# Two transformer blocks on one core: the scaling of the sixteen gate tiles moved from VectorE to GpSimd

## What is computed

```python
u = rms_norm(h, mix_pre_g[i])
proj = u @ w_in[i]
(q_a, c_kv, q_idx, k_idx, w_idx, q_h, f_h, i_h, g_h, gate_a, gate_b) = split_cols(proj)
...
merged = (jax.nn.sigmoid(gate_a + b_gate[i, :D]) * (y_a @ w_br_a[i])
          + jax.nn.sigmoid(gate_b + b_gate[i, D:]) * (y_b @ w_br_b[i]))
h = h + rms_norm(merged @ w_out[i], mix_post_g[i])
```

## Time and profile before

| | us |
|---|---|
| three runs | 2024.76, 2026.54, 2027.18 |
| median | 2026.54 |
| the profiled execution | 2031.31 |
| its span in the trace | 2029.4 |
| PE busy | 1861.8 (92%) |
| DVE busy | 1167.6 (58%) |
| ACT busy | 648.5 (32%) |
| POOL busy | 201.2 (10%) |

### The profile page before, as it was taken

One profiled execution on the slowest core, in us unless ns is written; L12 is line 12 of the kernel. 1 busy time (PEld: TensorE's weight loads), 2 busy tenths in 40 slices (PEclk: granted clock), 3 DMA queues, 4 the chain that ended last, 5 costly groups with the idle time before them and its releaser, 6 DMA issues.

```text
span 2029.4 us, 23515 instructions
## 1 busy us (share of the span) xinstructions
PE 1861.8 (92%) x8254; PEld 1489.2 (73%) x8254; DVE 1167.6 (58%) x1772; ACT 648.5 (32%) x960; POOL 201.2 (10%) x150
## 2 busy tenths in 40 slices
PE   5887989999999999999899998877789999999996
PEld 4665777777888888888677776666567788888874
DVE  6447658888534755532443776576683755452266
ACT  4333412222223222222333334444353322222242
POOL 3121000000000000000033344243000000000000
PEclk9888999999999999999899999977899999999997
DMA  3431222223222222323222331310152222232221
GB/s 136 79 67 42 73 80 89 92 92 101 100 98 83 93 93 97 103 100 100 78 83 73 114 129 59 114 68 32 47 161 83 73 96 101 93 119 100 92 71 54
DMA packets 55340, 180.61 MB, mean 89 GB/s; under 512 B 6216, under 2 KB 6984, under 8 KB 55272
## 3 DMA queue, kind: packets, MB, share of 16 engines
q1 hardware_dynamic: 43200, 157.07, 23.2%
q10 hardware_dynamic: 12072, 22.67, 4.0%
HBM read 167.65 MB, written 12.06 MB: 89 GB/s over the span
## 4 chain that ended last, share of the span: by engine, by line
PE 68%; DVE 19%; issue 6%; ACT 3%; DMA 2%; POOL 1%; DVEq 1%; ACTq 0%; SPq 0%; POOLq 0%
PE bank L721 16%; PE bank L722 16%; PE bank L723 16%; PE bank L743 2%; PE bank L744 2%; PE bank L809 2%; PE bank L745 2%; PE bank L810 2%; PE bank L811 2%; DMA raw<-in_w_proj 1%; DVE sq L1990 1%; PE bank L1078 1%; PE bank L789 1%; DVE w_lo L1711 1%; DVE chunk L1809 1%
## 5 line engine op out<-in xcount | busy, mean ns | idle before, releaser
L1142 ACT ACTIVATE w_hi<-raw 128x1024 fp32r<-128x1024 f32 (+2 forms) x281 | 304.4, 1087 | 742.7 <-PE bank L723 677.8
L721 PE MATMUL bank<-a_hi,w_hi 128*128 128x512 f32 x1272 | 504.1, 396 | 17.9 <-DVE w_lo L1711 7.7
L723 PE MATMUL bank<-a_hi,w_lo 128*128 128x512 f32 x1272 | 496.8, 391 | 0.0
L722 PE MATMUL bank<-a_lo,w_hi 128*128 128x512 f32 x1272 | 496.5, 390 | 0.0
L1711 DVE TENSOR_TENSOR w_lo<-raw,w_hi 128x1024 fp32r<-128x1024 f32 (+2 forms) x219 | 280.4, 1281 | 246.7 <-ACT w_hi L1142 234.2
L721 PEld LDWEIGHTS bank<-a_hi,w_hi 128*128 128x128 f32 x1272 | 239.9, 189 | 87.9 <-issue 19.7
L723 PEld LDWEIGHTS bank<-a_hi,w_lo 128*128 128x128 f32 x1272 | 239.7, 188 | 50.7
L722 PEld LDWEIGHTS bank<-a_lo,w_hi 128*128 128x128 f32 x1272 | 240.1, 189 | 49.4 <-issue 1.0
L633 POOL TENSOR_TENSOR w_lo<-raw,w_hi 128x1024 fp32r<-128x1024 f32 x54 | 130.5, 2419 | 1103.9 <-ACT w_hi L1142 1103.9
L721 PE MATMUL bank<-h_hi,w_hi 128*128 128x512 f32 x568 | 221.1, 389 | 0.2 <-DVE w_lo L1711 0.2
L723 PE MATMUL bank<-h_hi,w_lo 128*128 128x512 f32 x568 | 221.0, 389 | 0.0
(11 more groups left out here) (291 smaller groups left out, 2255.3 us busy)
## 6 DMA issues: line engine op xcount, KB each, us to landing
raw<-in_w_up SPq DMA_DIRECT2D x132, 512.0 KB, 3.4
raw<-in_w_down SPq DMA_DIRECT2D x48, 704.0 KB, 4.0
raw<-in_w_proj SPq DMA_DIRECT2D x59, 512.0 KB, 3.5
raw<-in_w_wo SPq DMA_DIRECT2D x8, 512.0 KB, 3.4
raw<-in_w_branch SPq DMA_DIRECT2D x16, 256.0 KB, 2.7
gates_in<-spill ACTq DMA_DIRECT2D x16, 256.0 KB, 3.0
raw<-in_w_out SPq DMA_DIRECT2D x8, 512.0 KB, 4.3
raw<-in_w_ple SPq DMA_DIRECT2D x8, 512.0 KB, 3.5
```

The costliest lines, as they stand in the source:

```text
L721: mm(dst[:, :], wh, hi[:, k, :], start=(first and c == 0), stop=False)
L722: mm(dst[:, :], wh, lo[:, k, :], start=False, stop=False)
L723: step = mm(dst[:, :], wl, hi[:, k, :], start=False, stop=(last and c == n - 1))
L1142: fn(w_hi[:, slot, 0:size], raw[:, slot, 0:size], ACT.Copy).then_inc(unit_high, 1)
```

## The change

The function `scale_gates` and its eight calls leave DVE's stream. POOL gets a loop at the end of its stream that waits for each pair's loads and multiplies the two tiles in place by `rstd_mix`, then raises `gates_scaled`. Loads, sigmoids and all semaphore counts stay as they were.

```diff
@@ -694,6 +694,13 @@
                 if e + 1 < HGRN_STEPS:
                     make_diff(e + 1)
 
+            for m in range(DC):
+                pool.wait_ge(gates_loaded[m % 2], 32 * (m // 2 + 1))
+                for n in range(2):
+                    slot = gates_in[:, 2 * (m % 2) + n, :]
+                    scaled = pool.tensor_tensor(slot, slot, rstd_mix[:, :], ALU.mult)
+                scaled.then_inc(gates_scaled, 1)
+
@@ -2305,16 +2312,7 @@
             dve.wait_ge(hg_loaded, 16 * HEADS)
-            def scale_gates(m):
-                dve.wait_ge(gates_loaded[m % 2], 32 * (m // 2 + 1))
-                for n in range(2):
-                    slot = gates_in[:, 2 * (m % 2) + n, :]
-                    scaled = v.tensor_tensor(slot, slot, rstd_mix[:, :], ALU.mult)
-                scaled.then_inc(gates_scaled, 1)
-
             for h in range(HEADS):
-                if h == HEADS - 1:
-                    scale_gates(0)
                 dve.wait_ge(head_sq, 7 + h)
@@ -2333,8 +2331,6 @@
                     chunk_ready, 1)
-                if m + 1 < DC:
-                    scale_gates(m + 1)
                 made(c)
```

## The result

The changed kernel took 2037.79 us (median of five runs, 2036.24 to 2039.06); the kernel before, its three runs and two more, 2026.54 (2024.76 to 2028.46). The ratio is 1.006, with a 95% interval of 1.0046 to 1.0074: 11.25 us by the medians, 9 to 15 by the interval. Slower was forecast, by 10.2 us.

What follows compares the result with a forecast made beforehand. The prediction took a DVE-ACT loop to pace the branch-stage rounds; rounds +6.9 us and head +3.3 us made 10.2, 2041.5 for a profiled execution, less 4.8 to the median: 2036.7 us, range 2030 to 2042.

Steps and rivals of the forecast that it cites:

- The bound: Branch-stage rounds: a closed loop through DVE and ACT sets the pace, PE holds no cushion, so changes reach the end time.
- The meeting: GpSimd and DVE instructions reading two SBUF operands take turns, one whole instruction each: +1.25 us a round in rounds 1 to 6.
- GpSimd is ready about 1.2 to 1.3 into the next round: Rounds: a pair's loads land about 3.2 us after `h_hi` starts, and GpSimd can then begin its scalings.
- The multiply: One GpSimd 128x512 multiply with two SBUF inputs takes 1.28 us (bounds 1.2 and 1.5), 2.56 a pair.
- -0.6 as the sigmoids needn't wait: Each round: sigmoids start right behind `h_hi` instead of behind DVE's scalings, saving 0.6 us; round 0 gains it too.
- The head: Ahead of the rounds: four GpSimd multiplies between DVE's paired reads delay PE's first diagonal by 3.3 us (bounds 0 and 5).
- The sum: Whole kernel: rounds +6.9 us and head +3.3 us give 10.2 us, 2036.7 us, 0.50% slower.
- DVE keeps its place: Rival: DVE's queued `chunk` goes ahead of GpSimd's second multiply, rounds stay 5.95 us, 2026, no change; chance 0.14.
- The two don't meet: Rival: in-place multiplies take no turn from DVE, 7 x 0.5 = 3.5 us faster, 2023; chance 0.06.
- Late loads: Rival: pairs start 2.05 us or more into the round, behind the second split; +0.6 a round, 2033; chance 0.10 (in part).
- The clock: Rival: PE's lower busy share in the rounds lowers its granted clock, costing some 8 us more, 2045; chance 0.08.

Runs made afterwards that it cites:

- three-slot pair: Rounds-only scaling on GpSimd with three pairs of gate slots instead of two; GpSimd starts after `chunk` (ratio 1.0005) or at the loads' landing (1.0044) against the kernel before.
- head-only kernel: Changed kernel with GpSimd scaling pairs 0 and 1 only, DVE the others in their old places: 2030.03 us, ratio 1.0012 to the kernel before.
- three-slot kernel with the late load: Kernel before with three gate slots, DVE scaling pair m+2 in round m, third pair's loads issued late; run twice: ratios 0.9993 and 0.9984.
- rounds-only kernel: Changed kernel with GpSimd scaling pairs 2 to 7 only, DVE pairs 0 and 1 as before: 2036.06 us, ratio 1.0052 to the kernel before.
- the halves: Changed kernel with each GpSimd multiply of 512 columns cut into two of 256: 2036.55 us, ratio 1.0048 to the kernel before.
- no scaling: Scaling of the gates left out on both engines, sigmoids wait for the loads alone: 2024.43 us, ratio 0.9987 to the kernel before.
- the kernel that waits for `chunk` with two slots: Rounds-only scaling on GpSimd, which also waits for the previous round's `chunk` before starting: 2039.31 us, ratio 1.007 to the kernel before.

## Why the prediction was right

**The bound.** Right: the rounds are a loop through DVE and ACT, PE idles in both kernels, and all of the rounds' +8.5 us reached the end (0.0 behind the stage).

**The meeting.** Right, in kind and in order: first split free, POOL, second split, POOL, `chunk`, gated products untouched. The three-slot pair shows it as the cause. Its size per round was set too small: +1.25 was forecast, and rounds 1 to 6 grew by 1.73, 1.54, 1.17, 2.00, 1.37 and 1.03, or 8.8 in all, where 7.5 stood. Three terms of the sum were off:
- "GpSimd is ready about 1.2 to 1.3 into the next round": it started 1.86 to 1.92 in (rounds 1, 2, 4), since it starts 4.1 us after `h_hi`'s start, not 3.2. The step took the landing of one round's loads, 2.8, for all. In the changed kernel the landings took 2.7 to 4.5 us, and POOL started within 0.1 us of the later of the two: for those issued in rounds 0, 1 and 2 the least, median and greatest time to landing are

```profile
DMA to landing us min/median/max: 3.4/3.5/3.7
...
DMA to landing us min/median/max: 2.7/3.2/3.7
...
DMA to landing us min/median/max: 2.7/2.9/3.1
```

and the second, issued 0.33 us after the first, took the greatest. The pair issued in round 2 landed in time: POOL started at 1.29 in round 3, and that round grew by 1.17, near the forecast's 1.25. (The kernel before had such spread too: 3.7 us in round 0.) Why some landings take longer isn't shown. Every tenth later than 1.41 pushes split and `chunk` back by as much: +0.45.
- The multiply: 1.2 us where I took 1.28: -0.16 for two. The row itself was right, an undisturbed multiply is recorded at 1.27 to 1.30 us; but instructions in a row start sooner than the records end (1.22 apart in the head), as DVE's 0.69 start 0.61 apart, and the sum took the one for POOL and the other for DVE. With the former this gives `h_hi` at 5.51 instead of 5.22; it was 5.45.
- "-0.6 as the sigmoids needn't wait": only -0.33, since the sigmoids stand 0.87 behind `h_hi`'s start (1481.94 to 1482.81) with ACT's two load issues in between: +0.27. The same term sits in round 0, 0.34 shorter instead of 0.6.

The Trainium skill's figure for a multiply (GPSIMD Engine Reference, section 3.1), 1.12 us by my estimate from it, lies as far below the 1.2 measured as the row's 1.28 above, and further from the recorded 1.27.

**The head.** +3.3 us to the first diagonal was forecast, +2.7 is there (15.49 against 12.78), +2.6 in the head-only kernel. The term that was too large is the multiply's cost to DVE, 4 x 1.28 = 5.1: DVE's four `a_lo` took 6.74 us where the earlier trace rows has 2.50, so 4.2, or 1.06 for each multiply. Less the pair that went (1.2) that is 3.0, and PE's slack took 0.3 of it. The figure is good to about 1 us only, since the three-slot kernel with the late load has its first diagonal at 12.84 in one execution and 13.87 in the other, with `a_lo` at 2.50 in both and PE's granted clock up to there 0.87 and 0.75.

```profile
1445.40 6.74 DVE L2311 TENSOR_TENSOR a_lo<-ya,a_hi 128x512 fp32r<-128x512 f32 x4 [4.18 <-ACT a_hi L1571]
```

**The sum.** 6.9 + 3.3 was forecast, 8.5 + 2.7 = 11.2 measured, and 11.25 by the medians: two errors of opposite sign, so that the total came out nearer (10.2) than its parts is in part luck. The agreement of trace and times shouldn't be read more closely either: the rounds-only kernel's ratio gives 10.5 us (7.7 to 13.2), its trace's rounds 7.8.

**The rivals.** *DVE keeps its place* fell with `chunk`'s 1.79 and again with the halves. *The two don't meet* fell too, and would not have paid 3.5 us, but 2.6 (no scaling). *Late loads* was half true: in rounds 1, 2 and 4 POOL started 0.6 us later than reckoned, and in full it happened once, when in round 6 POOL started at 2.71, behind the second split, and that round grew by 1.03, the least, though by more than the rival's 0.6, since the sigmoids then waited 0.5 for the second multiply. *The clock* fell below 0.9 in one round (0.78 in round 2), which at 7.71 us was no longer than its neighbour of 7.68: PE had slack there.

## What to carry to other kernels

Before work is moved from DVE to GpSimd, list which DVE instructions beside it read two SBUF operands and stand on the path; each can be held up for nearly a whole two-input GpSimd instruction (here 1.0 to 1.1 of its 1.2 us), however much time GpSimd has to spare. If it must run there, choose the time by a semaphore, which takes a buffer more, and once the buffer is there the old engine may do it at no cost to the rounds (39.25 us with DVE's scaling, 39.20 without any). For the moment at which an engine can use a load, take the landings of several rounds and the later of a pair, not one round's median.

## What the runs showed of the hardware that I had not expected

- A GpSimd multiply by a constant, one SBUF input, took 1.48 us for 128x512, longer than the two-input one at 1.2, and held DVE's paired reads up by 0 to about 0.4 us only.
- PE's granted clock in the head norms differs from one execution to the next, and moves the stage by up to 2.9 us. Two spreading matmuls of the changed kernel, the third and the fourth pair:

```profile
1462.09 1.13 PE L796 MATMUL bank<-diagonal,ones 128*128 128x512 f32 x2 [1.58 <-DVE diagonal L1665]
1464.80 1.12 PE L796 MATMUL bank<-diagonal,ones 128*128 128x512 f32 x2 [1.59 <-DVE diagonal L1665]
```

In the kernel before the same two read 2.04 and 2.07, and the way from the first diagonal to round 0 took 16.46 us, at a granted clock of 0.79, instead of 14.62 at 1.00. That isn't the change's doing: in the kernel that waits for `chunk` with two slots, whose head is that of before, they read 1.13 and 1.12 and the way took 14.62 too; and in the head-only kernel, whose head is that of the changed kernel, it took 17.53, at 0.71. What decides it isn't shown. This hid most of the head's loss in the changed kernel's trace (+0.87 to round 0 instead of +2.7).
